# Front of a hybrid attention and state-space layer reordered: u weights and token norm first, matrix set-up on VectorE, sample drive in 32-row pieces

## The chip, the cores and the metric

One core of a Trainium2 chip. The time is device microseconds of one execution of the whole program, the median of several runs. Matrix products run on TensorE (PE), element work on VectorE (DVE), ScalarE (ACT) and GpSimd (POOL); SyncE (SP) and ScalarE issue the DMAs, each on a queue of its own. PSUM has eight banks of 128 x 512 float32.

## The reference

One step of one layer, for 256 prompt tokens and 8 sample tokens of width 1024, in float32:

```python
proj = rms_norm(x, norm_mix) @ w_in                       # 1024 x 1280: q 512 | k 128 | v 128 | u 512
attn = window_attention(q, k, v, sinks)                   # window 128, ALiBi; samples use a cache of 128
# S5: 32 groups x 64 complex states, 16 inputs each
lam_bar = exp(lam * exp(log_step)); b_bar = (lam_bar - 1) / lam * b
x_t = lam_bar * x_(t-1) + b_bar u_t;  y = gelu(Re(c x) + d * u)
ssm = y * sigmoid(y @ w_glu + b_glu)
h = x + concat(rms_norm(attn), rms_norm(ssm)) @ w_out
h = h + moe(rms_norm(h))                                  # 32 experts, top 4, w_up 1024 x 2048, w_down 1024 x 1024
h = h + sigmoid(rms_norm(h) @ w_ple_gate) * (p @ w_ple_proj)
```

The outputs are the normed h, the new key and value windows and the last S5 states.

## The kernel before, in words

The program has a front (everything up to the output projection L832), a router, a loop over the 32 experts that streams 12 MB of weights for each, and a tail. Each engine has its own instruction list, written out by hand; it runs in order, and semaphores (`Z[...]`, `ld_...`) tie the lists together. A wait holds everything behind it on its engine.

The prompt is treated in 64 blocks of 4 steps (`BLOCKS`, `STEPS`). The S5 parameters are computed in 16-row form on DVE and ACT (L1390 to L1433, `R[...]`, among them Exp and Sin), turned by TensorE (L512) and copied by ACT to `pcols` (L1129, `par_sb`). DVE then builds powers of lambda (`lam`), `b_bar`, the drive matrices `e_bd` (L1474 to L1478) and half of the readout matrices `f_bd` (L1485 to L1489); GpSimd clears these buffers first (L422 to L428), computes the phase of each block (L436 to L439), the decay, and the other half of `f_bd` (L454 to L463). `turn_drive` (L544) transposes `e_bd` on TensorE, ACT copies it to `e_t` (L1164). The token norm is: ACT squares and roots (L1119, L1106), DVE scales (L1384), TensorE transposes (L506), DVE copies with the norm weights (L1439, `norm_sb`).

`project_u` (L539) makes u in PSUM banks 0 to 3; ACT spreads it to `u_blk` (L1150) and `u_s`. `drive` (L557) multiplies 8 of 16 tiles; `drive_samples` (L572) does the 8 sample tokens for all tiles, 2 x 16 products of 32 rows by 128 columns with 8 moving columns. `through_blocks` (L1497, on DVE) rotates, scans and rotates back one half. `within_blocks` (L581) makes the matrix within a block, copied by ACT (L1182), completed by DVE with the direct term (L1530) and laid out by ACT and GpSimd (L1186, L475). `project_one` (L623) makes k, v and four q slots in banks 6 and 7, copied by ACT (`qkv`, L1189); the third and later ones wait for a copied bank. SP loads the caches after the sixth of them, then the first expert's upward slabs.

`read_out` (L603) makes the S5 output in banks 2 and 3; ACT applies GELU on the way out in 32 pieces (`unit_input`, L1246). The rest of the front is attention for two blocks (`scores`, `biases`, `exps`, `p_transposes`, `values`), the sample attention, the gated unit (L764), the sums of squares of the S5 output (L771, `ssm_sums`), roots, scales and turns (`att_root`, `att_scale`, `att_turned`), and the output projection L832. w_out is loaded after the readout.

A matrix product in float32 leaves two MATMUL records in the profile, a transpose one.

## Time and profile before

| | us |
|---|---|
| median of 3 runs (1352.58 to 1356.2) | 1353.73 |
| the profiled execution | 1353.54 |
| its span, first to last instruction | 1351.8 |
| mean granted TensorE clock, share of full | 0.952 |
| busy: PE, DVE, ACT, POOL | 1245.0, 327.2, 209.9, 55.1 |

The page's 40 slices are 34 us each; the front takes the first five and a bit, the expert loop most of the others:

```profile
PE   4599678999999999999999999999999999999875
DVE  7942314112221111121221111111221111111132
ACT  3404712001010110101010110101110101100022
PEclk9869879989999999999999999999999999998878
DMA  8006413497999999999999999999999999999300
```

Each digit is the busy share of its slice in tenths; PEclk is the granted TensorE clock in tenths of full speed. The engines are uneven in the front and TensorE and the DMA engines are full in the expert loop.

### The profile page before, as it was taken

Reading aid. Unit: us, or ns where it says so; the run is one execution under the profiler, and the core shown is the slowest. Engines: PE = TensorE matmul, PEld = TensorE weight load, DVE = VectorE, ACT = ScalarE, POOL = GpSimd, SP = SyncE. Lnnn points to the kernel's source line nnn. Section 1 sums busy time; section 2 is a strip of 40 time slices with the busy share of each in tenths; the row PEclk is TensorE's granted clock in tenths of the full one; section 3 lists DMA queues with packets and bytes.
Section 4 is the critical chain, followed back from the end, with each engine's and each line's share of the span. In section 5 each row is a group of like instructions: output and inputs, shape, how many; then the busy total and the mean of one; then the engine's idle time right before and its main releaser. Section 6 shows DMA issues by size and latency. Waiting matters only on the chain.

```text
span 1351.8 us, 15552 instructions
## 1 busy us (share of the span) xinstructions
PE 1245.0 (92%) x5966; PEld 612.6 (45%) x5966; DVE 327.2 (24%) x553; ACT 209.9 (16%) x426; POOL 55.1 (4%) x70
## 2 busy tenths in 40 slices
PE   4599678999999999999999999999999999999875
PEld 3497566433434343434434343434344343434354
DVE  7942314112221111121221111111221111111132
ACT  3404712001010110101010110101110101100022
POOL 6600000000000000000000000000000000000000
PEclk9869879989999999999999999999999999998878
DMA  8006413497999999999999999999999999999300
GB/s 262 1 32 239 165 65 125 170 400 319 421 402 417 413 407 424 406 423 406 422 393 421 409 402 423 385 424 410 422 402 422 388 408 415 407 381 359 152 1 33
DMA packets 72238, 438.47 MB, mean 324 GB/s; under 512 B 13616, under 2 KB 16816, under 8 KB 21472
## 3 DMA queue, kind: packets, MB, share of 16 engines
q1 hardware_dynamic: 71632, 437.62, 79.6%
q10 hardware_dynamic: 576, 0.45, 0.1%
q8 instruction: 20, 0.33, 0.1%
q14 instruction: 10, 0.08, 0.0%
HBM read 436.67 MB, written 2.41 MB: 325 GB/s over the span
## 4 chain that ended last, share of the span: by engine, by line
PE 89%; DVE 5%; issue 2%; ACT 2%; DMA 0%; ACTq 0%; DVEq 0%
PE ps L943 38%; PE ps L960 18%; PE ps L929 10%; PE ps L899 5%; PE ps L832 2%; PE ps L1072 2%; PE ps L951 2%; PE ps L902 1%; PE ps L533 1%; PE ps L628 1%; PE ps L577 1%; PE ps L568 1%; PE ps L764 1%; PE ps L1015 1%; PE ps L969 1%
## 5 line engine op out<-in xcount | busy, mean ns | idle before, releaser
L943 PE MATMUL ps<-ring_up,region 128*64 128x512 f32 x2112 | 463.5, 597 | 2.6 <-issue 1.4
L943 PEld LDWEIGHTS ps<-ring_up,region 128*64 128x64 f32 x2112 | 164.1, 138 | 284.0 <-issue 282.1
L960 PE MATMUL ps<-ring_dn,region 128*64 128x512 f32 x1056 | 247.4, 623 | 12.4 <-issue 11.0
L1803 DVE TENSOR_SCALAR region<-ps 128x512 f32<-128x512 f32 x33 | 22.8, 691 | 715.1 <-PE ps L943 715.1
L960 PEld LDWEIGHTS ps<-ring_dn,region 128*64 128x64 f32 x1056 | 82.9, 143 | 163.6 <-issue 161.6
L929 PE MATMUL ps<-region,n_tok 128*128 128x128 f32 (+1 forms) x768 | 136.1, 307 | 0.0
L929 PEld LDWEIGHTS ps<-region,n_tok 128*128 128x128 f32 (+1 forms) x768 | 104.2, 187 | 41.2 <-issue 12.2
L1323 ACT ACTIVATE region<-region 128x512 f32<-128x512 f32 x33 | 20.8, 629 | 501.3 <-DVE region L1803 501.3
L1335 ACT ACTIVATE region<-ps 64x512 f32<-64x512 f32 x66 | 39.1, 592 | 270.4 <-PE ps L960 270.0
L899 PE MATMUL ps<-region 128*128 128x512 f32 (+1 forms) x136 | 68.7, 629 | 2.6 <-issue 1.3
L943 PE MATMUL ps<-region 128*64 128x512 f32 x264 | 62.7, 592 | 0.0
L1795 DVE TENSOR_TENSOR x_tok<-x_tok,ps 128x1024 f32<-128x1024 f32 x36 | 43.8, 1218 | 38.0 <-PE ps L899 35.8
L485 POOL COPY region<-kst 128x64 f32 (+1 forms) x33 | 7.8, 237 | 988.8 <-PE ps L943 988.7
L1325 ACT ACTIVATE region<-ps 128x512 f32<-128x512 f32 x33 | 19.7, 597 | 163.0 <-PE ps L951 163.0
L1781 DVE TENSOR_TENSOR region<-ps,vecs 128x512 f32<-128x512 f32 x32 | 22.1, 692 | 83.6 <-PE ps L929 83.6
L899 PEld LDWEIGHTS ps<-region 128*128 128x128 f32 (+1 forms) x136 | 23.9, 196 | 35.1 <-issue 33.8
L943 PEld LDWEIGHTS ps<-region 128*64 128x64 f32 x264 | 20.6, 137 | 36.0 <-issue 36.0
L832 PE MATMUL ps<-fb,ring_dn 128*128 128x264 f32 x128 | 31.6, 412 | 2.0 <-DVE fb L1631 2.0
L951 PE MATMUL ps<-kst,region 128*128 128x128 f32 x132 | 25.1, 314 | 5.7 <-DVE region L1810 5.7
L1072 PE MATMUL ps<-fb,ring_up 128*128 128x264 f32 x128 | 28.9, 387 | 0.4 <-DVE fb L1879 0.4
L832 PEld LDWEIGHTS ps<-fb,ring_dn 128*128 128x128 f32 x128 | 26.0, 205 | 7.0 <-issue 2.1
L951 PEld LDWEIGHTS ps<-kst,region 128*128 128x128 f32 x132 | 18.5, 208 | 21.5 <-DVE region L1810 19.6
(359 smaller groups left out, 824.0 us busy)
## 6 DMA issues: line engine op xcount, KB each, us to landing
ring_up<-in_w_up_dram SPq DMA_DIRECT2D x264, 1024.0 KB, 11.9
ring_dn<-in_w_down_dram SPq DMA_DIRECT2D x132, 1024.0 KB, 7.8
ring_up<-in_w_in_dram SPq DMA_DIRECT2D x4, 1280.0 KB, 9.9
ring_dn<-in_w_out_dram SPq DMA_DIRECT2D x1, 4096.0 KB, 20.9
ring_up<-in_w_ple_gate_dram SPq DMA_DIRECT2D x4, 1024.0 KB, 6.7
...
```

Source lines behind the costliest of these rows:

```text
L832: m = mm(bank(o % 4, T), w_out[:, k, o * P:(o + 1) * P], fb[:, k, :], start=(k == 0), stop=(k == KD - 1))
L899: m = mm(ps[:, SHARE_B[c][half], :], weights[rows_, t0:t0 + P], outputs(half), start=True, stop=True)
L929: m = mm(ps[:, X_B[k // 4], (k % 4) * P:(k % 4 + 1) * P], n_tok[0:nt, c, k * P:(k + 1) * P], sel[0:nt, c].rearrange("p a s -> p (a s)"), s ...
L943: m = mm(ps[64 * (q % 2):64 * (q % 2) + 64, q // 2, :], xe[:, k, slots] if k < UP else one_hot, w, start=(k == 0), stop=(k == UP))
L951: m = tr(ps[:, T_B, j * P:(j + 1) * P], by_row[:, j // 2, j % 2], ident)
L960: m = mm(ps[64 * half:64 * half + 64, O_B, :], act_t[:, f % 4, 64 * (f // 4):64 * (f // 4) + 64], ring_dn[:, f, 512 * half:512 * half + 51 ...
L1072: m = mm(bank(b_, T), w_gate[:, k, o * P:(o + 1) * P], fb[:, k, :], start=(k == 0), stop=(k == KD - 1))
L1323: f(sig, g_lim, ACT.Sigmoid, scale=ALPHA).then_inc(Z["sig_rdy"], 1)
L1335: m = f(out_e[C * a:C * a + C, half], ps[64 * half:64 * half + 64, 4], ACT.Copy)
L1781: V.tensor_tensor(xe[:, 4 * h:4 * h + 4], ps[:, (2, 5)[h]].rearrange("p (k s) -> p k s", k=4), col(vecs[:, V_FFN + 4 * h:V_FFN + 4 * h + 4 ...
L1795: V.tensor_tensor(xh, xh, ps[0:nt, b_:b_ + 2, :], ALU.add).then_inc(Z["cmb_read"], 1)
L1803: V.tensor_scalar(g_lim, bank(0), LIMIT, None, ALU.min).then_inc(Z["g_rdy"], 1)
```

## The change

- SP loads the seven vectors first and then w_in in two column parts, the u part (own semaphore `ld_wu`) before q, k and v. ACT issues the loads of C, B and the S5 states instead of the vectors, after its three parameter loads.
- ACT loads the Sqrt table ahead and takes each root right after its square; DVE scales and copies the tokens between the steps of the S5 parameters.
- GpSimd keeps the clearing of `f_bd` and `b_down` and its half of the lay copies. DVE clears `e_bd`, `m_flat` and the heads of `decay`, computes the phase and all of `f_bd`; ACT writes the decay and the first step of `f_bd`.
- TensorE: `project_u(0)`, then the parameters, then the other three u products, then all eight fills of `turn_drive`, both drives, the sample drive, `within_blocks`, and all six `project_one`. The sample drive is 2 x 16 x 4 products of 32 rows by 32 columns.
- ACT copies u in 16 pieces of 32 x 256 instead of 32 of 32 x 128, each group of four followed by two drive copies; both drives wait for the last of it (`us_sb`). `within_copies` stands ahead of all q, k, v copies.
- The readout is copied as it is, 8 pieces by ACT and 8 by DVE, and one GELU follows over all of it. `cache_transposes(1)` stands ahead of `values(0)`; `p_transposes(1)`, `values(1)` come directly after the gated unit.
- The squares of the attention output are taken early, its two roots in one instruction after the last S5 square; scales and turns of both blocks follow there.

```diff
@@ -316,16 +315,17 @@
 for c in range(2):
     sp.dma_start(x_tok[:, c], x_p[c * P:(c + 1) * P, :]).then_inc(ld_x, 16)
 sp.dma_start(x_tok[0:NB, 2], x_s).then_inc(ld_x, 16)
-for r, name in enumerate(("ssm_b_re", "ssm_b_im")):
-    sp.dma_start(b_raw[:, r], A[name][0].rearrange("(k g) p h -> (g p) k h", g=2)).then_inc(ld_b, 16)
-for r, name in enumerate(("ssm_c_re", "ssm_c_im")):
-    sp.dma_start(c_raw[:, r], A[name][0].rearrange("(k g) h p -> (g h) k p", k=4)).then_inc(ld_c, 16)
-for r, name in enumerate(("state_ssm_re", "state_ssm_im")):
-    sp.dma_start(rows[:, (10 + r) * P:(11 + r) * P],
-                  A[name][0].rearrange("b (k g) p -> (b k) (g p)", g=2)).then_inc(ld_x0, 16)
+r0 = 0
+for name, k in (("norm_mix", 8), ("norm_ffn", 8), ("norm_ple", 8), ("norm_attn_out", 4),
+                ("norm_ssm_out", 4)):
+    sp.dma_start(rows[r0:r0 + k, 0:P], A[name][0].rearrange("(k p) -> k p", p=P)).then_inc(ld_vec, 16)
+    r0 += k
+sp.dma_start(rows[r0:r0 + 4, 0:P], A["ssm_d"][0].rearrange("(k g) h -> k (g h)", k=4)).then_inc(ld_vec, 16)
+sp.dma_start(rows[r0 + 4:r0 + 8, 0:P], A["b_glu"][0].rearrange("(k p) -> k p", p=P)).then_inc(ld_vec, 16)
 w = A["w_in"][0].rearrange("(k p) n -> p k n", p=P)
-for k in range(0, KD, 2):
-    sp.dma_start(w_in[:, k:k + 2], w[:, k:k + 2]).then_inc(ld_win, 16)
+for arrived, cols in ((ld_wu, slice(D_IN - D_SSM, D_IN)), (ld_win, slice(0, D_IN - D_SSM))):
+    for k in range(0, KD, 4):
+        sp.dma_start(w_in[:, k:k + 4, cols], w[:, k:k + 4, cols]).then_inc(arrived, 16)
 sp.dma_start(sink_b, A["sinks"][0].partition_broadcast(P)).then_inc(ld_sink, 16)
 for b_ in range(NB):
...
@@ -417,59 +417,17 @@
     ins.then_inc(pool_step, 1)
     pool.wait_ge(pool_step, n[0])
-tt = nc.gpsimd.tensor_tensor
...
-    nc.gpsimd.memset(e_bd[r], 0.0).then_inc(Z["zeroed"], 1)
-for r in range(2):
-    nc.gpsimd.memset(f_bd[r], 0.0).then_inc(Z["zeroed"], 1)
...
-pool.wait_ge(Z["par_sb"], 1)
-magic = 12582912.0
-y, whole = (x.rearrange("p (i b) -> p i b", i=ST) for x in (cos_t, sin_t))
-turn = col(pcols[:, 5], BLOCKS)
-block = kst[:, K_IOTA:K_IOTA + BLOCKS].unsqueeze(1).to_broadcast([P, ST, BLOCKS])
-chain(tt(y, turn, block, ALU.mult))
-chain(nc.gpsimd.tensor_scalar(sin_t, cos_t, magic, None, ALU.add))
-chain(nc.gpsimd.tensor_scalar(sin_t, sin_t, -magic, None, ALU.add))
-tt(cos_t, cos_t, sin_t, ALU.subtract).then_inc(Z["phase"], 1)
...
-    for par in range(2):
-        g = slice(par * S, par * S + S)
-        chain(nc.gpsimd.tensor_copy(f_bd[r][g, :, 0, par], c_cc[g, r]))
-pool.wait_ge(Z["s5_sb"], 1)
-pool.wait_ge(Z["turned_ps"], 2)
-s1, s2 = (fb_flat[:, 1024 * a:1024 * a + 1024].rearrange("p (i j h) -> p i j h", i=ST, j=STEPS)
-          for a in range(2))
-tt(s1, every_step(c_cc[:, 0], STEPS), per_step(0, STEPS), ALU.mult)
-chain(tt(s2, every_step(c_cc[:, 1], STEPS), per_step(1, STEPS), ALU.mult))
-for par in range(2):
-    g = slice(par * S, par * S + S)
-    chain(tt(f_bd[0][g, :, 1:, par], s1[g], s2[g], ALU.add))
-nc.gpsimd.nop().then_inc(Z["f_sb"], 1)
 def lay(k, q):
...
@@ -522,7 +483,6 @@
                    group[:, par], start=True, stop=True)
 m.then_inc(Z["turned_ps"], 1)
 pe.wait_ge(ld_x0, 32)
-pe.wait_ge(Z["par_sb"], 1)
 for r in range(2):
     m = tr(ps[:, 6, r * P:(r + 1) * P], rows[:, (10 + r) * P:(11 + r) * P], ident)
...
+def turn_drive():
     pe.wait_ge(Z["e_bd_sb"], 2)
-    for f in range(4):
-        r, quad = f // 2, 2 * half + f % 2
-        n_ = 4 * half + f
-        if n_ >= 2:
-            pe.wait_ge(Z["e_sb"], n_ - 1)
+    for f in range(8):
+        r, quad = f // 2 % 2, f // 4 * 2 + f % 2
+        if f >= 2:
+            pe.wait_ge(Z["e_sb"], f - 1)
         for j in range(4):
-            m = tr(ps[:, 4 + n_ % 2, j * P:(j + 1) * P],
+            m = tr(ps[:, 4 + f % 2, j * P:(j + 1) * P],
                    e_bd[r][:, 4 * quad + j].rearrange("p k g h -> p (k g h)"), ident)
         m.then_inc(Z["e_ps"], 1)
 def drive(half):
     pe.wait_ge(Z["e_sb"], 4 * half + 4)
-    pe.wait_ge(Z["u_blk_sb"], half + 1)
+    pe.wait_ge(Z["us_sb"], 1)
     if half == 0:
         pe.wait_ge(Z["turned_sb"], 2)
...
-    pe.wait_ge(Z["us_sb"], 2)
     for r in range(2):
         for i in range(ST):
-            m = mm(ps[:, 4, (ST * r + i) * NB:(ST * r + i + 1) * NB], e_t[0:32, r, i], u_s[0:32, i],
-                   start=True, stop=True)
+            for p in range(0, P, 32):
+                m = mm(ps[p:p + 32, 4, (ST * r + i) * NB:(ST * r + i + 1) * NB], e_t[0:32, r, i, p:p + 32],
+                       u_s[0:32, i], start=True, stop=True)
...
@@ -633,6 +590,7 @@
     slot, b = (4, 5, 0, 1, 2, 3)[n_], 6 + n_ % 2
     if n_ == 0:
+        pe.wait_ge(ld_win, 32)
         pe.wait_ge(Z["x_states"], 1)
     if n_ >= 2:
...
-pe.wait_ge(Z["vec_sb"], 1)
 project_u(0)
-project_u(1)
...
-turn_drive(1)
 drive(1)
 drive_samples()
-project_one(0)
-project_one(1)
 within_blocks()
-for n_ in range(2, 6):
+for n_ in range(6):
     project_one(n_)
 kv_to_tokens()
...
 read_out(1)
 turn_states()
+cache_transposes(0)
 p_transposes(0)
-cache_transposes(0)
+cache_transposes(1)
 values(0)
-cache_transposes(1)
 scores(1)
 sample_scores()
 gated_unit()
-att_transposes(0)
+p_transposes(1)
 turn_sample_probs()
-p_transposes(1)
+values(1)
 sample_values()
-values(1)
 ssm_sums()
 sample_norm()
+att_transposes(0)
 att_transposes(1)
 turn_sample_outputs()
...
-for name, k in (("norm_mix", 8), ("norm_ffn", 8), ("norm_ple", 8), ("norm_attn_out", 4),
-                ("norm_ssm_out", 4)):
-    act.dma_start(rows[r0:r0 + k, 0:P], A[name][0].rearrange("(k p) -> k p", p=P)).then_inc(ld_vec, 16)
-    r0 += k
-act.dma_start(rows[r0:r0 + 4, 0:P], A["ssm_d"][0].rearrange("(k g) h -> k (g h)", k=4)).then_inc(ld_vec, 16)
-act.dma_start(rows[r0 + 4:r0 + 8, 0:P], A["b_glu"][0].rearrange("(k p) -> k p", p=P)).then_inc(ld_vec, 16)
+for r, name in enumerate(("ssm_c_re", "ssm_c_im")):
+    act.dma_start(c_raw[:, r], A[name][0].rearrange("(k g) h p -> (g h) k p", k=4)).then_inc(ld_c, 16)
+for r, name in enumerate(("ssm_b_re", "ssm_b_im")):
+    act.dma_start(b_raw[:, r], A[name][0].rearrange("(k g) p h -> (g p) k h", g=2)).then_inc(ld_b, 16)
+for r, name in enumerate(("state_ssm_re", "state_ssm_im")):
...
+    root(0, c)
+act.wait_ge(Z["vec_ps"], 1)
+f(vecs[:], bank(7, V_N), ACT.Copy).then_inc(Z["vec_sb"], 1)
 act.wait_ge(Z["par_red"], 3)
 f(R[3], R[9], ACT.Sin)
 f(R[15], R[9], ACT.Sin, scale=0.5).then_inc(Z["par_sin"], 1)
-act.wait_ge(Z["vec_ps"], 1)
...
-act.wait_ge(Z["par_ps"], 1)
-f(pcols, ps[:, 6, 0:6 * ST].rearrange("p (a b) -> p a b", a=6), ACT.Copy).then_inc(Z["par_sb"], 1)
 act.wait_ge(Z["turned_ps"], 1)
...
+for r in range(2):
+    for par in range(2):
+        g = slice(par * S, par * S + S)
+        m = f(f_bd[r][g, :, 0, par], c_cc[g, r], ACT.Copy)
+m.then_inc(Z["f_sb"], 1)
+act.wait_ge(Z["par_ps"], 1)
+f(pcols, ps[:, 6, 2 * P:2 * P + 6 * ST].rearrange("p (a b) -> p a b", a=6), ACT.Copy).then_inc(Z["par_sb"], 1)
+act.wait_ge(Z["s5_sb"], 1)
+by_tile = decay.rearrange("p (i b) -> p i b", i=ST)
+f(by_tile[:, :, 1:BLOCKS], col(mag[:, 1], BLOCKS - 1), ACT.Copy).then_inc(Z["phase"], 1)
 act.wait_ge(Z["s5_sb"], 2)
...
-        act.wait_ge(Z["e_ps"], n_ + 1)
-        f(e_t[:, r, 4 * quad:4 * quad + 4], ps[:, 4 + n_ % 2].rearrange("p (k n) -> p k n", k=4), ACT.Copy
-          ).then_inc(Z["e_sb"], 1)
-act.wait_ge(Z["phase"], 1)
+        m = f(u_blk[32 * k:32 * k + 32, q::4], ps[32 * q:32 * q + 32, 0:4, STEPS - 1 - k:SEQ:STEPS], ACT.Copy)
+    return m
+def drive_copy(n_):
+    r, quad = n_ // 2 % 2, n_ // 4 * 2 + n_ % 2
+    act.wait_ge(Z["e_ps"], n_ + 1)
+    f(e_t[:, r, 4 * quad:4 * quad + 4], ps[:, 4 + n_ % 2].rearrange("p (k n) -> p k n", k=4), ACT.Copy
+      ).then_inc(Z["e_sb"], 1)
+act.wait_ge(Z["phase"], 2)
 f(sin_t, cos_t, ACT.Sin, scale=6.283185)
 f(cos_t, cos_t, ACT.Sin, scale=0.5 * 6.283185).then_inc(Z["sines"], 1)
-block_copies(0)
-drive_copies(0)
-block_copies(1)
-drive_copies(1)
+act.wait_ge(Z["u_ps"], 4)
+for k in range(STEPS):
+    block_copies(k)
...
+    act.wait_ge(Z["att_ssq"], 2)
+    f(small[:, 84:86], small[:, 80:82], ACT.Sqrt, scale=1.0 / D_ATTN, bias=eps).then_inc(Z["att_root"], 1)
 def cache_copies():
...
-        for t in range(STEPS):
-            for q in range(4):
-                f(y_t[32 * q:32 * q + 32, 2 * half:2 * half + 2, t:SEQ:STEPS],
-                  by_tile[32 * t:32 * t + 32, :, q], ACT.Gelu_apprx_tanh)
-    act.wait_ge(Z["ypre"], 1)
-    f(y_t[:, :, SEQ:T], y_t[:, :, SEQ:T], ACT.Gelu_apprx_tanh).then_inc(Z["gelu"], 1)
+    act.wait_ge(Z["y_rot"], 2)
+    for t in range(2):
+        for q in range(4):
+            m = f(y_t[32 * q:32 * q + 32, :, t:SEQ:STEPS], by_step[32 * t:32 * t + 32, :, q], ACT.Copy)
+    m.then_inc(Z["ypre"], 1)
+    act.wait_ge(Z["ypre"], 3)
+    f(y_t, y_t, ACT.Gelu_apprx_tanh).then_inc(Z["gelu"], 1)
...
-qkv((0, 1))
 within_copies()
-qkv((2, 3, 4, 5))
+qkv()
 kv_tokens()
 exps(0)
 p_copies(0)
+unit_input()
 state_copies()
...
     act.wait_ge(Z["ssm_y"], c + 1)
     if c >= 2:
         act.wait_ge(Z["ssm_ssq"], c - 1)
     f(sq[:, c % 2], fb[:, 4 + c, :], ACT.Square).then_inc(Z["ssm_sq"], 1)
+att_root()
 act.wait_ge(Z["s_gps"], 1)
 f(s_small[0:64, 6:7], ps[0:64, 4, 0:1], ACT.Sqrt, scale=1.0 / D_ATTN, bias=eps[0:64]
...
 def halves(x):
     return x.rearrange("k (g p) -> k g p", g=2)
+for r in range(2):
+    V.memset(e_bd[r], 0.0).then_inc(Z["zeroed"], 1)
...
+norm_row(0, 0)
 chain(V.tensor_scalar(R[1], R[9], STEPS / (2.0 * np.pi), None, ALU.mult))
+norm_row(0, 1)
 chain(V.tensor_scalar(R[8], R[1], magic, None, ALU.add))
+norm_row(0, 2)
 chain(V.tensor_scalar(R[8], R[8], -magic, None, ALU.add))
 chain(V.tensor_tensor(R[1], R[1], R[8], ALU.subtract))
+dve.wait_ge(Z["vec_sb"], 1)
+normed(0)
 chain(V.tensor_tensor(R[8], l_re, l_re, ALU.mult))
 chain(V.tensor_tensor(R[7], l_im, l_im, ALU.mult))
+normed(1)
 chain(V.tensor_tensor(R[8], R[8], R[7], ALU.add))
+normed(2)
 chain(V.reciprocal(R[8], R[8]))
-norm_rows(0)
...
+place = kst[:, K_IOTA:K_IOTA + BLOCKS].unsqueeze(1).to_broadcast([P, ST, BLOCKS])
+chain(V.tensor_tensor(y, turn, place, ALU.mult))
+chain(V.tensor_scalar(sin_t, cos_t, magic, None, ALU.add))
+chain(V.tensor_scalar(sin_t, sin_t, -magic, None, ALU.add))
+V.tensor_tensor(cos_t, cos_t, sin_t, ALU.subtract).then_inc(Z["phase"], 1)
 f1, f2 = (wide(a, 1024).rearrange("p (i j h) -> p i j h", i=ST, j=STEPS) for a in range(2))
-dve.wait_ge(Z["turned_sb"], 1)
...
+by_step = ps[:, 2:4, :].rearrange("p n b -> p (n b)").rearrange("p (c q b) -> p c q b", c=4, q=4)
+def unit_input():
+    dve.wait_ge(Z["y_rot"], 2)
+    for t in range(2, STEPS):
+        for q in range(4):
+            m = V.tensor_copy(y_t[32 * q:32 * q + 32, :, t:SEQ:STEPS], by_step[32 * t:32 * t + 32, :, q])
+    m.then_inc(Z["ypre"], 1)
...
+unit_input()
 attended(0)
 biases(1)
 sample_bias()
 sample_own()
-att_scale(0)
-att_turned(0)
 spread_probs()
+attended(1)
 sample_outputs()
-attended(1)
 for c in range(KM):
     dve.wait_ge(Z["glu_sig"], c + 1)
     V.tensor_tensor(fb[:, 4 + c, :], y_t[:, c, :],
                     glu_s[:, c % 2], ALU.mult).then_inc(Z["ssm_y"], 1)
+att_scale(0)
 att_scale(1)
-att_turned(1)
+att_turned(0)
 sample_scaled()
 dve.wait_ge(Z["ssm_root"], 1)
 chain(V.reciprocal(sq[:, 0], sq[:, 1]))
+att_turned(1)```
```

## Rows read from the trace of the kernel before

**Rows 1.** The chain of waits, 130 to 182 us: start, length, what.
```profile
137.76 9.53 issue
147.29 10.11 PE ps L764 x32
...
173.03 0.32 ACT region L1290
...
181.48 18.53 PE ps L832 x70
```

**Rows 2.** Stretches: busy time (x instructions) by engine, granted clock, DMA share, GB/s.
```profile
core 0: us, PE busy (x) PEld busy (x) DVE busy (x) ACT busy (x) POOL busy (x), PEclk, DMA share, GB/s
...
500.00:700.00 200.00, 197.80 (x913) 83.73 (x911) 34.39 (x48) 21.95 (x33) 1.42 (x6) 0.99 1.00 411
...
65.00:70.00 5.00, 4.31 (x21) 3.91 (x19) 2.23 (x4) 1.20 (x2) 0.00 (x0) 0.50 0.01 3
```

**Rows 3.** DMA issues of SP in order of time: start, length, instruction.
```profile
3.01 4.74 SPq L320 DMA_DIRECT2D region<-in_ssm_b_im_dram  x1
...
17.25 6.13 SPq L333 DMA_DIRECT2D router_b<-in_b_router_dram  x1
```

**Rows 4.** Instructions of POOL, then of DVE, 0 to 121 us: start, length.
```profile
10.61 1.82 POOL L428 MEMSET region<- 128x2048 f32 x1
...
7.92 4.58 DVE L1401 TENSOR_SCALAR fb<-fb 16x128 f32<-16x128 f32 x1
...
22.89 0.28 DVE L1433 TENSOR_TENSOR fb<-fb 16x128 f32<-16x128 f32 x1
23.10 2.66 DVE L1439 TENSOR_TENSOR fa<-ps,vecs 128x512 f32<-128x512 f32 x6
...
32.06 0.96 DVE L1474 TENSOR_TENSOR n_tok<-region 128x768 f32<-128x768 f32 x1
32.94 3.10 DVE L1475 TENSOR_TENSOR n_tok<-region 128x768 f32<-128x768 f32 x1
...
56.79 0.69 DVE L1495 TENSOR_SCALAR region<-region 128x1024 f32<-128x1024 f32 x1
...
120.49 0.54 DVE L1581 MEMSET region<- 128x576 f32 x1
```

**Rows 5.** DVE, second half of the scan and sample states, 74 to 92 us.
```profile
74.21 1.22 DVE L1508 TENSOR_TENSOR n_tok<-ps,region 128x1024 f32<-128x1024 f32 x1 [6.90 <-PE ps L568]
...
83.31 0.68 DVE L1524 TENSOR_TENSOR fb<-n_tok 128x512 f32<-128x512 f32 x1
88.03 0.49 DVE L1640 COPY region<-ps 128x128 f32<-128x128 f32 x2 [4.04 <-PE ps L577]
...
91.39 0.38 DVE L1650 TENSOR_TENSOR region<-region 128x128 f32<-128x128 f32 x1
```

**Rows 6.** TensorE, products of the front: start, length, form, records.
```profile
47.46 3.79 PE L568 MATMUL ps<-final_g,ring_up 128*128 128x64 f32 x32 [0.69 <-ACT ring_up L1164]
...
67.08 7.09 PE L568 MATMUL ps<-final_g,ring_up 128*128 128x64 f32 x32 [0.69 <-ACT ring_up L1164]
74.10 13.82 PE L577 MATMUL ps<-region,ring_up 32*128 32x8 f32 x64
87.85 9.13 PE L533 MATMUL ps<-fa,ring_up 128*128 128x264 f32 x32
...
98.87 14.46 PE L628 MATMUL ps<-fa,ring_up 128*64 128x264 f32 x128
...
114.52 0.82 PE L598 MATMUL ps<-region,ring_dn 128*32 128x8 f32 x64
...
129.69 2.00 PE L705 MATMUL ps<-kv_tok,region 128*128 128x64 f32 x16 [0.30 <-ACT region L1216]
...
173.40 3.72 PE L771 MATMUL ps<-region,kst 128*128 128x264 f32 x8 [6.93 <-ACT region L1290]
```

**Rows 7.** ACT, copies and GELU of the front, 37 to 147 us.
```profile
37.17 4.45 ACT L1150 ACTIVATE final_g<-ps 32x128 f32<-32x128 f32 x16
...
44.15 0.60 ACT L1164 ACTIVATE ring_up<-ps 128x512 f32<-128x512 f32 x1 [1.57 <-PE ps L553]
...
100.39 3.81 ACT L1186 ACTIVATE region<-region 32x128 f32<-32x128 f32 x8 [0.81 <-DVE region L1530]
...
134.19 12.76 ACT L1246 ACTIVATE region<-ps 32x128 f32<-32x128 f32 x32
```

More of the change, by code:

```diff
@@ L74 @@
 PP_BANK = (6, 7, 0, 1, 2, 6, 7, 0)
-P_BANK = ((5, 6), (5, 7))
-V_BANK = (7, 6)
+P_BANK = (5, 6)
 UP, DN = 8, 4
```

187 lines of the change are left out of this document (88 added, 99 removed).

## The prediction, made before the changed kernel was run

> **What bounds the kernel now.** I read the page first: PE is busy for 92% of the span and the DMA share is full over most of it. The table of stretches says where: in the expert loop DMA engines and TensorE are both at their limit [rows 2]; nothing in the change touches that loop, and its first weights are fetched again only as the first expert uses its slabs. So the loop moves as a block, and the change is worth what it does to the moment at which the output projection (L832) starts, 181.48 us [rows 1]. All edits lie before it. The chain of waits of those 181 us shows short pieces that hop between DVE, PE and ACT: a latency chain, in which an engine's mean load says little. Two holes stand out: TensorE waits 9.53 us for the GELU and then runs the gated unit cold (10.11 us) [rows 1]; and from 65 us it runs at 1.2 GHz, half clock [rows 2], through drive, sample drive and part of the projections, where the same drive took 3.79 us at full clock and 7.09 at half [rows 6]. On DVE, instructions that meet a GpSimd one are stretched: a 16x128 tensor_scalar took 4.58 us and ended where a POOL memset ended; of two alike 128x768 products one took 0.96, the other 3.10 [rows 4].
>
> I follow one chain of milestones, in the trace's own time.
>
> **Start to parameter rows.** Before, L1433 begins at 22.89 [rows 4]. Now ACT issues nine DMAs, six of them the B, C and state loads with small elements, ahead of its first Exp. An issue costs about 0.44 us, so nine end at 0.77 + 9 x 0.44 = 4.75 if none blocks. On SP the second B load blocked for 4.74 us [rows 3]; I take the same block once on ACT (ACT free at about 9.5, as lower end no block, 4.75; the upper end is a rival below). A table load of 1.28 and the first Exp bring it to 11.0; DVE's seven short steps end at 13.2 with no POOL stall, since GpSimd has only 4 memsets left and DVE's own three (128x2048; 128x576 took 0.54 [rows 4], so about 1.9 each, 6.5 us in all from 0.8) end before. ACT: Exp, Sqrt table, then square and root by chunk at about 1.5 us each: roots at 14.6, 16.2, 17.6. DVE scales the three chunks behind them (0.75 each), does the three steps between, the six norm copies (2.66 [rows 4]) with 5 short steps: normalised tokens complete at 22.7 (before 25.8). Then reciprocal 0.95 and thirteen steps of about 0.28 us: parameter rows at 27.3, that is 4.2 us later than before. The u weights (2 MB of the 5) are wanted at 22.7; all of w_in was in by 26.5 before, so they cost nothing.
>
> **Matrices.** Before, from there to the first sample-drive turn was 20.0 us (23.0 to 43.0). Of it the norm copies are gone (2.7), and the stalls beside GpSimd: 3.10 - 0.96 on L1475 [rows 4], and five more of 0.1 to 0.9, 4.0 in all; two short squares are added (0.4); turning the parameters and their copy stay. 20.0 - 2.7 - 4.0 + 0.4 = 13.7, with a wait of 0.4 for the semaphores on three engines: 27.3 + 14.1 = 41.4. TensorE runs the u projections beside it (u0 before the parameters, three more to 39.0): hidden. **Phase.** The four wide phase steps move from POOL to DVE behind the e matrices: 2 x 1.2 (as the products of that width in the scan) [rows 5] + 2 x 0.69 [rows 4] = 3.8, at 45.2. ACT waits for that with everything behind it (Sin, block copies, drive copies), although u was ready at 39: a new wait. Sines 2.1: 47.3. The f matrices (9.9 us) follow on DVE and hide behind ACT.
>
> **Blocks and drive.** 32 block copies of 32x128 (4.45 us for 16, 0.278 each [rows 7]) become 16 of 32x256; I take 0.37 (ends 0.29, the pace of contiguous PSUM copies, and 0.42), 5.9. Eight drive copies, 0.60 each with the tail and 0.51 apart, 4.1 [rows 7], five small ones 1.0: 11.0, so us_sb at 58.3. Both drives now wait for it. Between, TensorE has only 32 turns spread over 17 us, so I take half clock: drive(0) 7.1 [rows 6] to 65.4, drive(1) to 72.5. Bounds: 3.8 each. **Scan.** A half runs from L1508 to L1524, 74.21 to 83.99, 9.78 [rows 5]: two of them, back to back now, end at 84.9. Sample states 3.75 (to 91.77, from 88.03) [rows 5], direct term 0.75, lay copies 3.85 [rows 7], then the first projection copy 0.4: 93.7. That order is new: within_copies stands ahead of all q/k/v copies on ACT, so the third projection, which waits for a copied bank, cannot start before 93.7.
> TensorE's side: sample drive. Before 64 records of 32 rows x 128 columns took 13.82 at half clock [rows 6]; now 256 records of 32x32. Nearest row: 64 records with 32 columns and 8 moving took 0.82, 12.8 ns each [rows 6], at full clock: 3.3, at half 6.6 (upper end: nothing saved, 13.8). 72.5 + 6.6 + within-blocks 3.9 + the first two projections 9.1 [rows 6] = 92.1: 1.6 us spare. So the sample drive's 7 us saved are off the path for most of their size; the scan and the lay copies are what is late next. Four q projections 14.46 [rows 6]: 93.7 + 14.4 = 108.1 against 113.4. Everything to the end of the readout keeps its pace (14.3): 122.4 against 127.6. **So far 5.2 us.**
>
> The Trainium skill (TensorEngine Tiling (Array Packing), Instruction Overhead) states some 60 cycles of overhead for each matmul and warns against tiling a dimension that is already small; it speaks against the pieces. By it 256 records at half clock would be 256 x 50 ns = 12.8 us, an estimate from that page, against my 6.6; L598's 12.8 ns per record disagrees with it.
>
> **Readout to output projection.** Times after the end of the readout, those of before in parentheses. ACT: probability copies to 2.6, eight output copies of 32x256 at 0.42 (the 32 GELUs of 32x128 took 12.76 [rows 7], gone) 3.4, Gelu table and one wide GELU 2.4, state copies 0.7, first cache copy 0.6: 9.7. The GELU is ready at 8.4 (19.5), but TensorE is in order and now has cache_transposes(1) ahead of values(0): it waits until 9.7 for ACT's first cache copy, a second new wait. values(0) cold 4.0 (2.00 warm [rows 6]) with the turn 0.9: 14.6; scores, biases and reduction bring the second maximum at 21.4, Exp to 25.5 (27.2); the gated unit runs meanwhile, 19.7 to 26.9. p_transposes(1) 27.0 (30.4), values(1) and sample values end at 36.0 (38.9); ssm_y at 37.5 (39.6). State stores 2.1, then no table loads before the squares (two were there): squares at 41.6 (45.4) [rows 1], ssm_sums 3.7 [rows 6], 45.7 (49.5). Now the cost at the end: a Sqrt table load, root, two scales, two turns and two copies all lie after the sums: 6.3 where 4.3 stood. Output projection at 52.0 (53.8): **1.8 us**. w_out lands 21 us after the readout, so it stays hidden, at a margin of 30 us.
>
> **Sum.** 5.2 + 1.8 = 7.0. The profiled execution's own time is 1353.54 for a span of 1351.8, within 0.2 of the median 1353.73. 1353.7 - 7.0 = **1346.7 us**.
>
> **Rivals.** (A) ACT's queue does not block, or TensorE is at full clock in the drives: 4.0 and 3.3 us more. For it: SP's block came behind larger loads. Against: 2 x 2048 small elements are on ACT's ring too. With one or both, 1343 to 1339, say 1341. (B) The 32-row pieces pay per instruction and the sample drive stays at 13.8: TensorE reaches the third projection at 99.3 instead of 93.7, 5.6 back: 1352.3. For it: four times the instructions; against: L598. (C) Slower: ACT's DMA issues block again and again. Each us past 9.5 passes to the roots, the parameter rows and so to the end. Three blocks of SP's longest, 6.13 [rows 3], instead of one of 4.74 free ACT at 4.75 + 18.4 = 23.2, less 1.3 of ordinary issues, 21.9: 12.4 later, 1359.1. It decides where ACT is free later than 16.5. Against it: with the big loads on SP's own ring ACT's ring holds only 0.6 MB. The Trainium skill (DMA: Bandwidth & Descriptors, Queues, rings and completion order) says that a DMA engine serves its queue rows in turn, packet by packet; by that rule ACT's small elements also share time with SP's w_in, which would lengthen their block, and no row here shows two loaded rings at once. (D) The gains sink into new waits: half clock lasts through scores and gated unit (10.11 instead of 7.2), block and output copies are at their upper bounds: 3 + 1.6 lost, 1351.3.
>
> **Chances.** Forecast 0.48, A 0.22, B 0.09, C 0.10, D 0.11. Range to 1355, toward C, and down to 1338.5 for A: it takes in the bounds (A's 4.0 + 3.3, copies 1.3). A measurement of this kernel can tell 0.3%, 4.1 us, from no change: faster means below 1349.7. The forecast's own range, 1343 to 1350.5, is nearly all faster; A all; B and D within 0.3%; of C three quarters are slower. Faster 0.68, same 0.24, slower 0.08.
>
> **What will show it.** Right: ACT's first Exp near 11.0 (near 7 is A, over 18 is C); e matrices ready near 41, ACT idle until 45 for the phase; drive from 58 at half clock; sample drive 6 to 7 us; the third projection held by ACT's copy near 94; projections done near 108; TensorE idle about 7.5 us after the readout behind cache_transposes(1); ssm_sums followed by 6 us before L832, which starts near 174.5. The prediction is wrong if the expert loop itself changes its length, or if the chain bends to TensorE between 72 and 94.

## The result, and the profile after

| | before | after |
|---|---|---|
| median (15 runs each, same chip), us | 1354.69 (1349.02 to 1357.84) | 1357.98 (1356.32 to 1361.82) |
| ratio after / before, 95% interval | | 1.0035 (1.0021 to 1.005) |
| profiled execution and its span, us | 1353.54, 1351.8 | 1358.6, 1356.8 |
| mean granted clock | 0.952 | 0.946 |
| output projection starts, us | 181.48 | 190.30 |

The prediction was 1346.7 us, and faster; the kernel became slower by 3.3 us. The front, which I had forecast 7.0 us shorter, is 8.8 us longer.

The lines of the page after the change (TensorE's busy tenths in 40 slices of 34 us, and its granted clock):

```profile
PE   2689778989999999999999999999999999999875
PEclk9769679989999999999999999999999999998888
```

TensorE's first slice holds 2 tenths where it held 4; the clock is lower in the second slice (7 tenths for 8) and in the fifth (6 for 8). The stretch inside the expert loop answers to [rows 2]: nothing changed there.

```profile
500.00:700.00 200.00, 197.06 (x913) 84.84 (x915) 35.82 (x51) 22.55 (x34) 1.43 (x6) 0.99 1.00 410
```

**Where it starts.** ACT's queue from the first microsecond on (start, length, instruction):

```profile
3.51 0.55 ACTq L1050 DMA_DIRECT2D region<-in_ssm_b_re_dram  x1
4.08 5.11 ACTq L1050 DMA_DIRECT2D region<-in_ssm_b_im_dram  x1
9.23 8.39 ACTq L1052 DMA_DIRECT2D fb<-in_state_ssm_re_dram  x1
17.64 0.91 ACTq L1052 DMA_DIRECT2D fb<-in_state_ssm_im_dram  x1
18.59 1.28 ACT L1069 ACT_TABLE_LOAD   x1 [18.59 <-issue]
```

Issuing nine loads took ACT 18.59 us. The second B load blocked it for 5.11 us, as on SP before (4.74 [rows 3]), and then the first state load for another 8.39. I had ACT free at 9.5; before the change it was free at 5.7. Everything after that follows late.

**The chain behind it**, last parameter row, phase on DVE, ACT's wait for it, drive, sample drive, q projections:

```profile
36.00 0.28 DVE L1419 TENSOR_TENSOR fb<-fb 16x128 f32<-16x128 f32 x1
...
49.91 1.23 DVE L1463 TENSOR_TENSOR region<-region,kst 128x1024 f32<-128x1024 f32 x1
...
53.88 1.06 ACT L1125 ACTIVATE region<-region 128x1024 f32<-128x1024 f32 x1 [9.96 <-DVE region L1466]
...
67.36 13.89 PE L525 MATMUL ps<-final_g,ring_up 128*128 128x64 f32 x64 [2.09 <-ACT ring_up L1121]
81.18 3.58 PE L534 MATMUL ps<-region,ring_up 32*32 32x8 f32 x251
...
103.06 16.31 PE L585 MATMUL ps<-fa,ring_up 128*64 128x264 f32 x128 [5.74 <-ACT region L1153]
```

**Between readout and output projection** TensorE runs in order (start, length, operation, idle time before it and its releaser):

```profile
144.77 1.11 PE L680 MATMUL ps<-kst,fa 128*128 128x128 f32 x4 [9.33 <-ACT region L1191]
145.68 3.52 PE L661 MATMUL ps<-kv_tok,region 128*128 128x64 f32 x16
149.12 5.67 PE L618 MATMUL ps<-region 64*128 64x256 f32 x16
154.72 3.58 PE L687 MATMUL ps<-region 128*64 128x129 f32 x16
158.23 7.39 PE L720 MATMUL ps<-region,ring_up 128*128 128x264 f32 x32
...
179.99 3.94 PE L727 MATMUL ps<-region,kst 128*128 128x264 f32 x8 [5.38 <-ACT region L1250]
...
190.30 2.10 PE L784 MATMUL ps<-fb,ring_dn 128*128 128x264 f32 x4 [2.46 <-DVE fb L1618]
```

The 9.33 us are the new wait behind `cache_transposes(1)`; values, scores and sample scores then run at half clock, and the gated unit, which had paid for the idle time before with 10.11 us [rows 1], is warm again. So the cold stretch was moved, not removed. The clock of that stretch:

```profile
144.70:158.20 13.50, 13.43 (x52) 11.22 (x52) 6.12 (x12) 2.73 (x6) 0.00 (x0) 0.51 0.71 282
```

A granted clock of 0.51 is the 1.2 GHz level, for 13.5 us in which TensorE had work at 13.43 of them, after the 9.33 us of idleness.

**Front and whole.** The front lost 8.8 us, the span only 5.0. The last combine, at the end of the expert loop, explains 3.7 of the difference. It ran at half clock in the trace of before and at full clock in that of after:

```profile
1285.34 3.03 PE L899 MATMUL ps<-region 64*128 64x512 f32 x4 [1.29 <-ACT region L1329]
1288.30 1.97 PE L902 MATMUL ps<-region 64*64 64x512 f32 x4
1290.20 3.78 PE L899 MATMUL ps<-region 64*128 64x512 f32 x4
```

```profile
1293.98 1.95 PE L851 MATMUL ps<-region 64*128 64x512 f32 x4 [1.28 <-ACT region L1290]
1295.87 1.08 PE L854 MATMUL ps<-region 64*64 64x512 f32 x4
1296.87 1.98 PE L851 MATMUL ps<-region 64*128 64x512 f32 x4
```

That belongs to the execution and not to the change: in the second trace of the kernel before, the last experiment, the same combine is at full clock.

### The profile page after: what moved, and what is told of

It is laid out like the page before. It is cut to its first block, busy times and chain, and to the rows that moved or that the text cites. A ratio compares the mean times of both kernels' runs of the same rounds, so it can differ in the third digit from the quotient of the medians.

```text
span 1356.8 us, 15894 instructions
## 1 busy us (share of the span) xinstructions
PE 1239.3 (91%) x6158; PEld 608.7 (45%) x6158; DVE 327.5 (24%) x574; ACT 200.7 (15%) x385; POOL 19.8 (1%) x51
## 3 DMA queue, kind: packets, MB, share of 16 engines
q10 hardware_dynamic: 5968, 1.08, 0.5%
## 4 chain that ended last, share of the span: by engine, by line
PE 87%; DVE 5%; ACT 4%; issue 2%; ACTq 2%; DVEq 0%
PE ps L895 38%; PE ps L912 18%; PE ps L881 10%; PE ps L851 5%; PE ps L784 2%; PE ps L1024 2%; PE ps L903 2%; PE ps L854 1%; PE ps L585 1%; ACTq L1052 1%; PE ps L967 1%; PE ps L921 1%; PE ps L720 1%; PE ps L567 1%; PE ps L661 1%
## 5 line engine op out<-in xcount | busy, mean ns | idle before, releaser
L912 PE MATMUL ps<-ring_dn,region 128*64 128x512 f32 x1056 | 247.3, 623 | 12.4 <-issue 11.0
L851 PE MATMUL ps<-region 128*128 128x512 f32 (+1 forms) x136 | 65.9, 606 | 2.6 <-issue 1.3
L1024 PEld LDWEIGHTS ps<-fb,ring_up 128*128 128x128 f32 x128 | 24.2, 190 | 4.5 <-DVE fb L1877 0.5
## 6 DMA issues: line engine op xcount, KB each, us to landing
ring_up<-in_w_up_dram SPq DMA_DIRECT2D x264, 1024.0 KB, 11.9
```

What stands on the lines that cost most here:

```text
L851: m = mm(ps[:, SHARE_B[c][half], :], weights[rows_, t0:t0 + P], outputs(half), start=True, stop=True)
L912: m = mm(ps[64 * half:64 * half + 64, O_B, :], act_t[:, f % 4, 64 * (f // 4):64 * (f // 4) + 64], ring_dn[:, f, 512 * half:512 * half + 51 ...
L1024: m = mm(bank(b_, T), w_gate[:, k, o * P:(o + 1) * P], fb[:, k, :], start=(k == 0), stop=(k == KD - 1))
```

## The experiments

Theory 1: the blocked DMA issues on ACT cost the front 13 us and hide a reordering that gains. The main rival, theory 2: the reordering itself costs, through phase, sines, in-order waits and pieces. The first nine were repeated, each beside the kernel before on the same chip; e1 to e4 stood on one chip, e5 to e8 on a second, the others on a third, so medians of different groups compare through their ratios. "ACT free" is the start of ACT's first table load, "drive" the start of the drive products (47.46 before, 67.36 after), "projection" the start of the output projection (181.48 before, 190.30 after), all in us of the run's own trace.

| kernel | median, us | ratio to before, interval | ACT free | drive | projection |
|---|---|---|---|---|---|
| e1_loads_back | 1344.73 | 0.9933 (0.9911 to 0.9955) | 5.7 | 54.26 | 178.43 |
| e2_swap_only | 1366.4 | 1.0094 (1.0061 to 1.0127) | 21.8 | 59.48 | 199.92 |
| e3_tail_only | 1354.83 | 1.0014 (0.9985 to 1.0042) | 5.6 | 46.99 | 187.0 |
| e4_whole_pieces | 1359.93 | 1.0048 (1.0023 to 1.0072) | 19.1 | 67.15 | 191.94 |
| e5_states_first | 1348.82 | 0.9976 (0.9948 to 1.0004) | 10.1 | 58.22 | 181.91 |
| e6_cache_first | 1338.4 | 0.9883 (0.9839 to 0.9927) | 5.5 | 55.3 | 165.41 |
| e7_sines_late | 1337.99 | 0.9886 (0.9845 to 0.9926) | 5.7 | 49.06 | 172.08 |
| e8_qkv_first | 1339.49 | 0.99 (0.9859 to 0.994) | 5.6 | 54.04 | 168.66 |
| e9_all_four | 1325.22 | 0.9771 (0.9746 to 0.9797) | 5.5 | 47.12 | 154.28 |
| e10_win_after | 1344.26 (one run) | | 10.8 | 58.9 | 182.31 |
| e11_before_again | 1349.24 (one run) | | 5.6 | 47.19 | 180.21 |

**The queues put back.** In the changed kernel, B, C and state loads go back to SP and the vectors to ACT:

```diff
-    sp.dma_start(rows[r0:r0 + k, 0:P], ...).then_inc(ld_vec, 16)      # 7 of them
+    sp.dma_start(b_raw[:, r], ...); sp.dma_start(c_raw[:, r], ...); sp.dma_start(rows[:, ...], ...)
-    act.dma_start(c_raw[:, r], ...); act.dma_start(b_raw[:, r], ...); act.dma_start(rows[:, ...], ...)
+    act.dma_start(rows[r0:r0 + k, 0:P], ...).then_inc(ld_vec, 16)
```

> The changed kernel with one part undone: the C, B and state loads are issued by SP and the seven vectors by ACT, as in the kernel before; w_in stays in its u part and its rest. Theory 1 (ACT's blocked DMA issues hold the front): ACT is free at about 5.7 us instead of 18.6, its first Exp starts near 7.2 instead of 19.9, the roots then wait for x, and every milestone up to L784 (190.3) comes 12 to 13 us earlier, near 178; median near 1358.0 - 12.5 = 1345.5. Theory 2 (the front bends to another chain at once: the u weights, now behind the B loads on SP, or TensorE): at most 4 us, 1354 or more.

The drive starts 13.1 us earlier and the output projection 11.9; the median falls by 13.3 us against after, and below before. So the blocked issues did cost the front 12 us. Against before, the trace shows a front only 3.05 us shorter, while the median is 10 us lower: of the 9.5 us between the two spans the other 6.5 lie in the loop (see the last experiment). What the reordering gains in the front is therefore hardly more than traces of equal instructions differ by (up to 2.6 us, see the run with the part after the readout alone).

**The exchange alone**, the mirror of the first: the kernel before, with nothing but the two groups of loads exchanged.

```diff
-    sp.dma_start(b_raw ...); sp.dma_start(c_raw ...); sp.dma_start(rows[:, ...] ...)
+    sp.dma_start(rows[r0:r0 + k, 0:P], ...)
-    act.dma_start(rows[r0:r0 + k, 0:P], ...)
+    act.dma_start(c_raw ...); act.dma_start(b_raw ...); act.dma_start(rows[:, ...] ...)
```

> The kernel before with only the exchange of the loads: SP issues the seven vectors, ACT the C, B and state loads. Theory 1: ACT is free near 18 instead of 5.7, but 4.6 us of the later Exp are covered by the DVE stall beside GpSimd that it replaces; parameter rows 8 us later, L832 near 189.5, median near 1354.7 + 8 = 1362.7. Theory 2 (the parameter chain had slack behind w_in, which arrived at 26.5): 3 us or less, under 1358.

```profile
4.04 5.24 ACTq L1098 DMA_DIRECT2D region<-in_ssm_b_im_dram  x1
9.30 11.93 ACTq L1100 DMA_DIRECT2D fb<-in_state_ssm_re_dram  x1
...
21.75 1.28 ACT L1112 ACT_TABLE_LOAD   x1 [21.75 <-issue]
```

Here the state load blocks for 11.93 us, with the four w_in parts of before on SP's ring: the exchange alone costs 0.9%, and the front 18.4 us. That is more than I had expected (ACT free near 18, projection near 189.5, 1362.7 us), in part because this block is longer than in the changed kernel. Both directions agree in sign and in the place.

**The part after the readout alone.** The kernel before, with the new order between readout and output projection only (plain copies by two engines and one GELU, `cache_transposes(1)` early, roots at the end).

```diff
-cache_transposes(0)
+cache_transposes(0); p_transposes(0); cache_transposes(1)
 values(0)
-unit_input as 32 GELUs on ACT, behind cache_copies
+unit_input ahead of state_copies and cache_copies: 8 + 8 copies, one GELU
```

> The kernel before with only the part after the readout changed (readout copied in 16 pieces by ACT and DVE and one GELU, cache_transposes(1) ahead of values(0), the new order of probabilities and values, roots at the end). The prediction's sum gives 1.8 us less than before: 1352.9, L832 at 179.7. The reading of the changed trace (pieces at 0.62 us instead of 0.42, TensorE idle for 9.3 us behind cache_transposes(1) and then at half clock through values and scores) gives readout to L832 56.4 us where 53.8 stood: L832 near 184.1, median 1357.3.

```profile
141.32 1.12 PE L721 MATMUL ps<-kst,fa 128*128 128x128 f32 x4 [9.33 <-ACT region L1228]
```

The stretch takes 56.8 us (before 53.8, forecast 52.0) with the same 9.33 us wait as after. The timing can't tell it from no change; the trace shows a loss of 3 us in place, where I had written a gain of 1.8. The projection is 5.5 us later than before, because this trace already reaches the end of the readout 2.6 us later (its first drive took 4.94 us instead of 3.79), with instructions that are the same up to there. One trace's milestones scatter by that much.

**The sample drive as whole products**, 32 of 32 x 128 instead of 128 of 32 x 32:

```diff
-            for p in range(0, P, 32):
-                m = mm(ps[p:p + 32, 4, ...], e_t[0:32, r, i, p:p + 32], u_s[0:32, i], ...)
+            m = mm(ps[:, 4, ...], e_t[0:32, r, i], u_s[0:32, i], ...)
```

> The changed kernel with the sample drive as before, 32 products of 32 rows by 128 columns instead of 128 of 32 by 32. In the changed trace the pieces took 5.3 us and TensorE then waited 5.7 us for ACT before the third projection, so if the pieces are off the path: sample drive 13.8, TensorE reaches the third projection 2.8 us late, its clock no longer falls in the wait (projections 14.4 instead of 16.3): 1358.0 + 1 = 1359. If each us saved in the sample drive reached the end: 8.5 more, 1366.5.

```profile
80.96 13.82 PE L533 MATMUL ps<-region,ring_up 32*128 32x8 f32 x64
...
106.32 14.46 PE L584 MATMUL ps<-fa,ring_up 128*64 128x264 f32 x128
```

The pieces save 8.5 us of TensorE (13.82 against 5.3, from 81.18 to 86.5), but the output projection moves by 1.6 only, within that scatter. With whole products TensorE fills the 5.74 us for which it otherwise waits for ACT's copy, and it stays warm: the q projections take 14.46 instead of 16.31.

**State loads first on ACT's queue:**

```diff
-    act: c_re, c_im, b_re, b_im, state_re, state_im
+    act: state_re, state_im, c_re, c_im, b_re, b_im
```

> The changed kernel with the six large loads still on ACT's queue, in the order states, C, B instead of C, B, states: nothing stands behind the second B load. If a load of many small elements blocks only the issue that follows it (8.39 us in the state load behind the B loads), ACT is free when the second B load is issued, near 10 us instead of 18.6, and all milestones come 8 to 9 us earlier than in the changed kernel: L784 near 182, median 1349.5. If the block is a matter of the queue's total load, ACT is free no earlier than 16 and the median stays above 1355.

```profile
2.16 0.45 ACTq L1048 DMA_DIRECT2D fb<-in_state_ssm_re_dram  x1
...
5.03 5.07 ACTq L1053 DMA_DIRECT2D region<-in_ssm_b_im_dram  x1
10.13 1.28 ACT L1069 ACT_TABLE_LOAD   x1 [10.13 <-issue]
```

The second B load blocks in either order (5.07 here, 5.11 in after). The state loads take 0.45 and 0.68 ahead of it and were blocked behind it: it is not the load that blocks, but what already stands in front of it. With one block instead of two the output projection is 8.4 us earlier. This is the arrangement that my sum had assumed ("the same block once": free at 9.5, here 10.1), and the run gives 1348.8 where the sum gave 1346.7. That the times are so near is luck: the output projection starts at 181.91 and not at 174.5, and this trace's unchanged stretch is 10 us shorter than that of before (1042.9 and 1053.1).

**w_in held back.** SP starts w_in only when ACT's state loads have landed:

```diff
+sp.wait_ge(ld_x0, 32)
 for arrived, cols in ((ld_wu, ...), (ld_win, ...)):
```

> The changed kernel, but SyncE starts the loads of w_in only after ScalarE's state loads have landed, so that while ScalarE issues its loads the other ring carries only tokens and vectors. Theory 1 (the issue of the first state load blocks 8.39 us because w_in's packets share the DMA engines with the small elements in front of it): that issue takes some 5 us or less, ScalarE is free near 14 to 15 us instead of 18.6, while the u projections start late because w_in is late. Theory 2 (the block depends only on what stands on ScalarE's own ring): the issue takes 8.4 us again and ScalarE is free at 18.6. The time as a whole is no measure here, since w_in is 20 us late: about 1365.

```profile
4.07 4.95 ACTq L1051 DMA_DIRECT2D region<-in_ssm_b_im_dram  x1
9.05 1.24 ACTq L1053 DMA_DIRECT2D fb<-in_state_ssm_re_dram  x1
...
10.80 1.28 ACT L1070 ACT_TABLE_LOAD   x1 [10.80 <-issue]
```

The landing times of two loads (size, us from issue to landing), after, and then with w_in held back:

```profile
region<-in_ssm_b_im_dram ACTq DMA_DIRECT2D x1, 128.0 KB, 23.6
fb<-in_state_ssm_re_dram ACTq DMA_DIRECT2D x1, 64.0 KB, 16.8
```

```profile
region<-in_ssm_b_im_dram ACTq DMA_DIRECT2D x1, 128.0 KB, 7.9
fb<-in_state_ssm_re_dram ACTq DMA_DIRECT2D x1, 64.0 KB, 3.0
```

With the other ring nearly empty the 8.39 us become 1.24, and the same B load lands after 7.9 us instead of 23.6. So there are two blocks of different kind: some 5 us at the second B load, with w_in on SP's ring (5.11, 5.07) or without it (4.95), and a second one that is long only while SP's ring carries w_in and what stands behind it. What the first one waits for, no run here shows. The Trainium skill (DMA: Bandwidth & Descriptors, Queues, rings and completion order) says that a DMA engine takes its queue rows in turn, a packet of each; these landing times agree with it. That the late w_in would make the kernel slow, as I had written, was wrong: SP issues it at 12.40 instead of 5.52, the u projections start at 23.75 instead of 31.53, and the output projection at 182.31 instead of 190.30. The one execution's 1344.26 says less: its unchanged stretch is among the shortest here (1042.9 us), and its front is 3.9 us longer than with the loads back on SP.

**Three waits of the new order, each taken away on top of the first repair** (e1_loads_back). First, state and cache copies ahead of the GELU on ACT:

```diff
+state_copies()
+cache_copies()
 unit_input()
-state_copies()
-cache_copies()
```

> The kernel with the loads back on their queues (e1_loads_back), with state_copies and cache_copies of ACT ahead of unit_input. Theory: TensorE's 9.3 us idle behind cache_transposes(1) and its half clock after it set the stretch from the readout to L784 (56.9 us): values(0) then starts 3 us after the readout, the second maximum comes before the GELU, the gated unit ends near 21 us after the readout instead of 32, and the stretch falls to 45 to 48; median 1344.7 - 10 = 1335. Rival (the stretch hangs on ACT's Exp and sigmoid chain): 52 or more, 1340 or more.

```profile
124.98 0.65 PE L680 MATMUL ps<-kst,fa 128*128 128x128 f32 x4 [1.96 <-ACT region L1191]
125.47 1.90 PE L661 MATMUL ps<-kv_tok,region 128*128 128x64 f32 x16
...
131.00 1.99 PE L687 MATMUL ps<-region 128*64 128x129 f32 x16
```

The wait shrinks from 9.33 to 1.96 us, the values run warm (1.90 instead of 3.52), and the stretch from readout to output projection takes 44.1 us instead of 56.9. The median, forecast at 1335, falls only to 1338.4: this trace has a longer loop (1053.1 us) than that of e1_loads_back (1046.6). Second, ACT's wait for the phase and the sines behind the u copies:

```diff
-act.wait_ge(Z["phase"], 2); f(sin_t, ...); f(cos_t, ...)      # ahead of block_copies
+act.wait_ge(Z["phase"], 2); f(sin_t, ...); f(cos_t, ...)      # behind us_sb
```

> e1_loads_back with ACT's wait for the phase and its two sines moved behind the last u copy (us_sb). Theory: the phase that DVE now makes behind the e matrices holds ACT from 36.8 to 40.6 us and the sines add 2; the block copies start at 35.3, where u is ready, and the drive at 47 instead of 54.3; L784 7 us earlier, 171.4; median 1338. Rival: the second scan half or the f matrices on DVE take over: 3 us or less, 1342.

The drive starts at 49.06 instead of 54.26, and the output projection 6.4 us earlier. Third, the first two k/v copies ahead of the within-block copies:

```diff
+qkv((0, 1))
 within_copies()
-qkv((0, 1, 2, 3, 4, 5))
+qkv((2, 3, 4, 5))
```

> e1_loads_back with ACT's copies of the first two projections ahead of within_copies, as in the kernel before. Theory: TensorE waits 5.1 us for the first of these copies and restarts at half clock (17.2 us for the four q products instead of 14.4); both go, the q products end near 99.5 instead of 107.2, the readout then waits for nothing new: L784 7.7 us earlier, 170.7; median 1337. Rival: the readout waits for the lay copies, which end at 90 already, or for the scan: under 3 us.

```profile
83.19 14.46 PE L585 MATMUL ps<-fa,ring_up 128*64 128x264 f32 x128
```

No idle time is left ahead of the q projections (5.07 us in e1_loads_back), and they run at full clock (14.46, not 17.24). The output projection comes 9.8 us earlier. So theory 2 holds as well, though not for the pieces: each of these three positions, which the new order brought, costs more than the 3.05 us that the front of e1_loads_back had gained.

**All four together:**

> The changed kernel with four repairs together: the C, B and state loads back on SyncE and the vectors back on ScalarE; ScalarE's phase wait and sines after the u copies; q/k/v copies 0 and 1 ahead of the within-block copies; the cache copies ahead of the GELU. The output projection starts at 178.4 us with the first repair alone; the others gave 6.4, 9.8 and 12.8 us on top of it one by one. Theory 1 (they lie in different stretches or shorten waits that follow one another, so they add): output projection at 149.5, span and median about 29 us below the 1344.7 us of the loads alone, 1316. Theory 2 (overlap: what the sines give before the drive is taken back, since the projections then run at half clock or DVE's matrices and scan are late next): the sum before the readout is 10 rather than 16 us, output projection at 155 and median near 1322. Theory 3 (with the readout 23 us earlier the caches, loaded behind the sixth projection, come late and TensorE waits for them in the first cache turn): output projection near 160, with a DMA named as the end of the wait, median near 1328.

The output projection starts at 154.28, 24.2 us before e1_loads_back and 27.2 before the kernel before; the three steps one by one had given 13.0, 6.4 and 9.8, in sum 29.2. Before the readout they add (14.9 of 15.5 us). Behind it 47.7 us stand where cache_first alone had 44.1, and the same work is cold:

```profile
110.30 0.66 PE L680 MATMUL ps<-kst,fa 128*128 128x128 f32 x4 [1.97 <-ACT region L1192]
...
113.02 5.67 PE L618 MATMUL ps<-region 64*128 64x256 f32 x16
118.62 3.70 PE L687 MATMUL ps<-region 128*64 128x129 f32 x16
```

Scores and sample scores took 3.2 and 1.99 us in e6_cache_first, behind an equally long wait of 1.96 us. So what is missing from the sum is granted clock, not a wait; a DMA (theory 3) is named in no wait there. Why the same work was cold behind the same wait in one trace and warm in the other, no run shows. Theory 2 had named about this place (155) and time (1322), but by an overlap before the readout, which didn't come. The kernel takes 1325.22 us, 2.3% below before: it beats both.

**The kernel before once more:**

> The kernel before once more, unchanged, for a second trace of it. Theory 1 (the length of the expert loop and of the last combine differ between executions with the granted clock, whatever the front does): the front ends at 181.5 us again, the loop takes 967 to 974 us and the last combine may be up to 4 us shorter than in the first trace. Theory 2 (the loop's length belongs to the kernel): 974.1 and 79.0 us as in the first trace.

From its first expert product to the last projection's start this second trace has 1049.9 us where the first had 1053.1. The last combine is warm in it (1.95, 1.08 and 1.98 us). Over all traces of this study the length ranges from 1042.9 to 1053.1 with the same instructions: 1049.5 in after, 1042.9 in e3_tail_only, 1046.6 in e1_loads_back, 1053.1 in e9_all_four. The lengths are not spread evenly: three traces have 1042.9, one 1046.6, five 1049.4 to 1049.9, and the four with a cold last combine 1053.1. The two traces of the kernel before differ by 3.2 us, most of it the combine; a short loop of this kernel is in neither, though among 29 of its executions with a median of 1354.99 us two took 1342.05 and 1343.3. Part of it shows at once in the granted clock of the loop's first 30 us (before, then e3_tail_only; the loop ahead of the last combine takes 974.1 and 967.7 us):

```profile
251.40:281.40 30.00, 26.45 (x102) 8.61 (x104) 3.65 (x6) 1.23 (x2) 0.24 (x1) 0.83 0.82 320
```

```profile
257.00:287.00 30.00, 26.46 (x123) 9.10 (x125) 3.64 (x6) 2.80 (x5) 0.24 (x1) 1.00 0.89 355
```

So a span from one trace says little about 3 us of front; medians of many runs and the milestones within the front say more. These scatter too: in this trace the output projection starts at 180.21, 1.3 us earlier than in the first. Whether a kernel's front also shifts the odds of a long or short loop stays open: medians moved by 10 us for e1_loads_back, whose front is 3 us shorter than that of before, and by 6.3 us from it to e6_cache_first (on another chip), whose front is 13 us shorter again. No run here separates this from chance.

## Why the prediction was wrong, point by point

**The step that failed** is the first: "I take the same block once on ACT (ACT free at about 9.5 ...)". ACT was free at 18.6. The rows I had showed SP's blocks [rows 3], two of them, and I counted one of them once; the second depends on what the other ring carries, which no row of before showed, and which rival C named. The argument against C ("with the big loads on SP's own ring ACT's ring holds only 0.6 MB") took the load on ACT's own ring for the limit, where e10_win_after shows that the other ring's load sets the second block. C had "decides where ACT is free later than 16.5" and a price of 12.4 us for 21.9; the trace gave 18.6. Its mechanism was only half as I had put it: two blocks, the second longer than any on SP, and not three of SP's longest. That its time, 1359.1, lies 1.1 us above the median is luck: by C's own rule the 9.1 us past 9.5 give 1355.8, and the rest is made up by terms that C didn't have. The range also ended at 1355, short of C's own time.

**From there to the parameter rows** everything took the forecast time: the last row at 36.0 instead of 27.3, the 9.1 us of ACT less 0.4. DVE's three clearings took 1.76 us each (forecast 1.9) from 1.26 to 7.3, beside GpSimd's. **Matrices and phase:** e matrices at 49.9 for 41.4, phase steps 1.23, 0.69, 0.69, 1.23 for the forecast 3.8 us in all; the two alike products now take 0.96 and 0.95 against 0.96 and 3.10 [rows 4]. ACT waited 9.96 us for them; that wait with the sines behind it costs 6.4 us, as e7_sines_late measured beside e1_loads_back; the prediction has it as a new wait, without a price of its own. **Blocks and drive:** a 32 x 256 copy took 0.38 (0.37), us_sb fell at 67.3, 9.0 late, and both drives 13.89 at half clock (2 x 7.1). **Sample drive:** 251 records in 3.58 us are 14 ns each, and 256 spanned 5.3 us with a hole of 1.48, for my 6.6; the clock there was granted at 0.50. Rival B is out. The Trainium skill (TensorEngine Tiling (Array Packing), Instruction Overhead) gives some 60 cycles of overhead for each matmul, and the prediction's 12.8 us by it counted the 256 records. A float32 product leaves two of them, so by the rule the 128 products are 128 x 50 ns = 6.4 us at half clock, an estimate from that page, against the measured 5.3. So neither this run nor L598, where 32 products took 0.82 us, 25.6 ns each, speaks against the rule as clearly as the prediction has it. The Trainium skill's warning in the same section against tiling a dimension that is already small doesn't bear on the pieces either: the dimension divided was the 128 columns. That the saving lies off the path was right: whole products move the output projection by 1.6 us.

**Third projection:** held by ACT's first copy, as forecast, at 103.06 for 93.7. Here a small term was missed: 5.74 us of idle time (forecast 1.6; TensorE was early, with the sample drive 1.3 quicker than I took and the first two projections 7.39 for 9.1 [rows 6]) put the q projections to half clock at their start, 16.31 instead of 14.46. With it the readout ended at 133.7 instead of 122.4, 11.3 us late: 9.1 from ACT, 1.9 from that restart and 0.3 of small terms.

**Readout to output projection:** forecast 52.0, measured 56.6. Two terms were mis-sized. The output copies of 32 x 256 took 0.62 us (4.93 for 8), where I took 0.42, hardly more than the 0.40 of one 32 x 128 GELU [rows 7]; twice the columns took half as long again. With that ACT's first cache copy came 1.3 us late and TensorE's wait was 9.33, not 7.5. And I gave the cold restart to the values alone: scores (5.67, 3.2 when warm) and sample scores (3.58, 1.99 when warm) were at half clock too. Wait, scores and sample scores make 1.3 + 2.5 + 1.6 = 5.4, of which 0.8 came back (values 3.52 for 4.0, smaller steps). The end with roots, scales and turns behind the sums was right: from the end of `ssm_sums` (183.93) to 190.30, 6.4 us for 6.3. What stood in the text as "a second new wait" was as dear as the loads: e6_cache_first shows that 13.0 us hang on it and its cold restart, e1_loads_back 11.9 on the loads.

**The sum**, then: 9.1 (ACT) + 2.2 (to the readout's end) + 4.6 (behind it) = 15.9 us, against 174.5 forecast and 190.3 measured. Of the 8.8 us that the front lost, the traces' spans hide 3.7, by a last combine that happened to be warm. Had the first step held, the other two terms would still have eaten the gain: with the state loads first ACT is free at 10.1, the output projection starts at 181.91, no earlier than before, and the ratio 0.9976 can't be told from no change. That is near rival D, gains that sink into new waits, though not by all it named: scores were at half clock and the output copies long, but the gated unit was warm (7.39) and the block copies took 0.38. So the call "faster" rested on both steps, and both failed.
